# Expert weights of the second and third layer in runs of 16 KB a partition

## The chip, the core and the metric

One core of one Trainium2 chip. The time is that of one execution of the whole program on the device, in microseconds; the median of several runs is given, and less is better. The core has TensorE (PE), VectorE (DVE), ScalarE (ACT), GpSimd (POOL) and SyncE (SP), and 16 DMA engines that all queues share. Each engine works through its own instructions in order and meets the others by semaphores.

## What is computed

Three layers of a model on 256 tokens (and 256 of context), D = 1024, all in fp32. Each layer ends in 16 experts, and these are what the change touches:

```python
# second layer ("layer 1"): each token goes to two of 16 experts
def expert_block(args):
    xblk, e = args
    hid = jax.nn.silu(xblk @ w_gate[e]) * (xblk @ w_up[e])
    return hid @ w_down[e]
...
# third layer ("layer 2"): each expert takes its 32 best tokens
    top_aff, top_idx = lax.top_k(jnp.swapaxes(aff, 1, 2), cap)
    xe = jax.vmap(lambda hb, ib: hb[ib])(h, top_idx)
    hid = jax.nn.silu(jnp.einsum('becd,edf->becf', xe, w_e_gate)) * jnp.einsum('becd,edf->becf', xe, w_e_up)
    ye = jnp.einsum('becf,efd->becd', hid, w_e_down) * top_aff[..., None].astype(h.dtype)
```

Each `w_gate[e]`, `w_up[e]`, `w_down[e]` is 1024 x 1024, so an expert reads 12 MB of weights for at most 64 (layer 1) or 32 (layer 2) rows of tokens. The first layer ("layer 0") has experts of the same size; the change leaves their weights as they are.

## The kernel before

All weights go through one list, `W`, of pieces of at most 2 MB. `W.add` (L263 to L327) says which part of a weight a piece is and in what shape: `cols(w, n, k0, k, width)` takes `k` chunks of 128 rows and puts row 128 c + p on partition p, chunk c. An expert's matrix is two pieces, `h` = 0 and 1, of `k` = 4 chunks and the full width of 1024: on a partition, four rows of 4 KB each, which lie 128 rows apart in HBM. Layer 1 takes its pieces expert by expert in the order of `PAIRS` (gate 0, gate 1, up 0, up 1, down 0, down 1); layer 2 in four groups of four experts, all gates of a group, then all ups, then all downs. So 96 pieces each.

`W.place` gives each piece a place in SBUF: the ring of five, and in layer 1 four more (nine), in layer 2 three of the ring, four more, and one that serves once (eight). `sync_pieces` (L384) issues the DMAs from SP, in the order of the list, each after the piece that was in its place has been used up:

```python
            if before is not None and W.rows[before][1] == "pe":
                sp.wait_ge(*consumed(before))
...
            sp.dma_start(dst, src).then_inc(landed(n)[0], 16)
```

`consumed` is counted by TensorE after the last matmul on a piece.

Layer 1 does one expert at a time. The rows of tokens lie in `H`; TensorE picks an expert's 64 with a matrix of ones (`PS<-SM,H`), ACT copies them to `xeT` (L1912), TensorE multiplies them by gate into bank 0 and by up into bank 1 (`PS<-ring,xeT`, 32 matmuls a matrix of 512 columns, and each in two halves of 16, one a piece), ACT makes `hid` = silu(bank 0) (L1917), DVE multiplies bank 1 into it (L1942), TensorE turns `hid` (L1899), DVE copies it out as `hidT` (L1944), and TensorE multiplies by down (`PS<-ring,hidT`). Between up and the turning of `hid` TensorE picks the rows of the next expert. `H` was made before, from the turned-back activations in PSUM, by ACT (L1735).

Layer 2 does the same by groups: silu at L4030, the product at L4057, turned at L4010, copied out at L4060. Its token rows are split in two parts, `HH` (`H_high`, ACT, L3895) and `HL` (`H_low`, DVE, L3936), and a matrix of ones `SS` picks from both into `XE`, all before the first expert.

There are two more loops (the functions `late_...`, around L2014) for experts of layer 1 with more than 64 tokens; here they have no turn.

Outside the experts the kernel saves the turned activations to HBM and loads them back once, as one DMA of 128 partitions with 16 KB each: `act.dma_start(HT.rearrange("p c t -> p (c t)"), HD)` (L1231). It is issued from ACT.

Of the kernel before, what the change touches and what calls it, by code (L numbers as in the profile page):

```python
# [6 lines left out]
P = 128  # L7
D = 1024
NS = 5
SLOT = 8 * 512  # L10
F32 = mybir.dt.float32
# [3 lines left out]
ALU = mybir.AluOpType  # L15
ACT = mybir.ActivationFunctionType
# [154 lines left out]
def program(nc, I, out):  # L171
# [54 lines left out]
    def bank(i, n=1):  # L226
        return PS[:, i * 512:(i + n) * 512]
# [31 lines left out]
    W = Pieces()  # L259

    def cols(w, n, k0=0, k=8, width=512):
        return w[k0:k0 + k * P, n:n + width].rearrange("(c p) n -> p c n", p=P)

    ada, win, wo = I["ada_w"], I["even_w_in"][0], I["even_w_out"][0]
    moe = {"g": I["moe_w_gate"], "u": I["moe_w_up"], "d": I["moe_w_down"]}

# [32 lines left out]
    moe1 = len(W.rows)  # L299
    for e in range(16):  # L300
        for m, h in PAIRS:
            W.add((1, e, m, h), cols(moe[m][1, e], 0, k0=512 * h, k=4, width=D), "pe", k=4, width=D)
    end1 = len(W.rows)
    w2 = I["w_in_2"][0]
    W.add(("dt", 0), cols(w2, 4608, width=48), "pe", width=48)
# [16 lines left out]
    for g in range(4):  # L322
        for m in "gud":
            for e in range(4 * g, 4 * g + 4):
                for h in range(2):
                    W.add((2, e, m, h), cols(last_experts[m][0, e], 0, k0=512 * h, k=4, width=D), "pe", k=4, width=D)
    end2 = len(W.rows)  # L327
    W.place(range(NS), 0, end0)
    W.place(range(NS), end0, end1, extra=(5, 6, 7, 10), first=moe1 + NS)
# [1300 lines left out]
    def routed(layer, chunks, BL, zeroed, resume):  # L1630
        wide = BL == P
# [98 lines left out]
        def route_scalar():  # L1730
            def rows(ts):
                for t in ts:
                    c, g = divmod(t, 2)
                    act.wait_ge(*row_turned(t))
                    act.copy(H[:, c, 512 * g:512 * g + 512], bank(2 + t % 6)).then_inc(row_made.sem, 1)  # L1735

            ready_table(ACT.Sigmoid)
            act.wait_ge(*logits(0))
            act.activation(aff, bank(1)[:, 0:N], ACT.Sigmoid).then_inc(chance.sem, 1)
            rows(range(2 * nch))  # L1740
# [92 lines left out]
        def near_experts():  # L1833
# [80 lines left out]
            def near_scalar(m):  # L1914
                i = m % 2
                act.wait_ge(*weights(m, "g", 1)[2])
                act.activation(hid[i], bank(0), ACT.Silu).then_inc(silu.sem, 1)  # L1917
                if m < 15:
                    take_scalar(m + 1)
                act.wait_ge(*share_turned(m))  # L1920
                act.copy(shares_T[i], bank(1)[:, 0:2 * P]).then_inc(share_taken.sem, 1)
# [11 lines left out]
            def near_vector(m):  # L1933
                i = m % 2
                if m < 15:
                    if m:
                        dve.wait_ge(*x_turned(m - 1))
                    pick(m + 1, firsts)
                weigh(m)
                dve.wait_ge(*weights(m, "u", 1)[2])  # L1940
                dve.wait_ge(*silu(m))
                dve.tensor_tensor(hid[i], hid[i], bank(1), ALU.mult).then_inc(hidden.sem, 1)  # L1942
                dve.wait_ge(*h_turned(m))
                dve.tensor_copy(hidT[i].rearrange("p (h j) t -> p j h t", h=2),  # L1944
                                bank(3).rearrange("p (j h t) -> p j h t", j=4, h=2)).then_inc(h_taken.sem, 1)
                dve.wait_ge(*weights(m, "d", 1)[2])
                dve.wait_ge(*gate_taken(0))
                dve.tensor_tensor(yo[i], bank(2), gate_twice, ALU.mult).then_inc(y.sem, 1)
# [55 lines left out]
            def late_sync(m):  # L2004
                expert = nc.sync.value_load(OE[0:1, m:m + 1], min_val=0, max_val=15)
                if m == 0:
                    sp.wait_ge(*late_sent(2 * nch - 1))
                    sp.wait_ge(*consumed(end1 - 1))
                if m > 1:
                    sp.wait_ge(*late_x_turned(m - 2))  # L2010
                sp.dma_start(late_xe[m % 2][0:BL, :], XP[(m + 16) * BL:(m + 17) * BL, :]).then_inc(late_xe_in[m % 2].sem, 16)
                for k, (mt, h) in enumerate(PAIRS):
                    if k >= NS:
                        sp.wait_ge(*late_used(6 * m + k - NS))  # L2014
                    elif m:
                        sp.wait_ge(*late_used(6 * m - 6 + (k if k else NS)))
                    v = moe[mt][layer].rearrange("e (c p) n -> p e c n", p=P)
                    sp.dma_start(ring_t[:, k % NS * SLOT:(k % NS + 1) * SLOT].rearrange("p (e c n) -> p e c n", e=1, c=4),
                                 v[:, bass.ds(expert, 1), 4 * h:4 * h + 4, :]).then_inc(late_in[k % NS].sem, 16)

            def late_tensor(m):
                i = m % 2
# [16 lines left out]
            def late_scalar(m):  # L2039
                i = m % 2  # L2040
                act.wait_ge(*late_x_turned(m))
                act.copy(xeT[i], chunked(bank(3), 8)).then_inc(late_x_taken.sem, 1)
                act.wait_ge(*late_piece(m, "g", 1)[2])
                act.activation(hid[i], bank(0), ACT.Silu).then_inc(late_silu.sem, 1)
                act.wait_ge(*late_y(m))
                for h in range(2):
                    act.dma_start(YP[(m + 16) * 64:(m + 17) * 64, 512 * h:512 * h + 512],
                                  yo[i][64 * h:64 * h + 64, :]).then_inc(late_stored[i].sem, 16)
                act.wait_ge(*late_stored[i](2 * (m // 2) + 1))

            def late_vector(m):
                i = m % 2
                dve.wait_ge(*late_piece(m, "u", 1)[2])
                dve.wait_ge(*late_silu(m))
                dve.tensor_tensor(hid[i], hid[i], bank(1), ALU.mult).then_inc(late_hidden.sem, 1)
                dve.wait_ge(*late_h_turned(m))
                dve.tensor_copy(hidT[i].rearrange("p (h j) t -> p j h t", h=2),
                                bank(3).rearrange("p (j h t) -> p j h t", j=4, h=2)).then_inc(late_h_taken.sem, 1)
                dve.wait_ge(*late_piece(m, "d", 1)[2])
                if m > 1:  # L2060
                    dve.wait_ge(*late_stored[i](2 * (m // 2) - 1))
                dve.tensor_tensor(yo[i], bank(2), gate_twice, ALU.mult).then_inc(late_y.sem, 1)
# [1825 lines left out]
    def choice_scalar():  # L3888
        ready_table(ACT.Exp)
        act.wait_ge(*shifted(0))  # L3890
        act.activation(af, af, ACT.Exp).then_inc(af_exped.sem, 1)
        for t in range(4):
            c, g = divmod(t, 2)
            act.wait_ge(*row_turned(t))
            act.copy(HH[:, c, 512 * g:512 * g + 512], bank(ROW_BANKS[t])).then_inc(row_made.sem, 1)  # L3895
        for i in (1, 3, 5, 7):
            k = XE_BANKS[i]
            act.wait_ge(*xe_made(i))
            act.copy(XE[:, k, :], bank(k)).then_inc(odd_taken.sem, 1)

    def choice_vector():
# [30 lines left out]
        for t in range(4):  # L3932
            c, g = divmod(t, 2)
            sl = slice(512 * g, 512 * g + 512)
            dve.wait_ge(*row_made(t))
            dve.tensor_tensor(HL[c][:, sl], bank(ROW_BANKS[t]), HH[:, c, sl].bitcast(F32), ALU.subtract).then_inc(row_low.sem, 1)  # L3936
        dve.wait_ge(*picked(1))
        for c in xc:
            dve.tensor_tensor(SW[:, c, :, :], SS[:, c, :, :].bitcast(F32), a3[:, c, :].unsqueeze(2).to_broadcast([P, 16, 32]),
# [82 lines left out]
    def experts_scalar():  # L4022
# [4 lines left out]
        for g in range(4):  # L4027
            for h in range(2):
                act.wait_ge(*consumed(W.at[2, 4 * g + 3, "g", 1]))
                act.activation(hid[g % 2][:, h * 512:h * 512 + 512], bank(4 + h), ACT.Silu).then_inc(silu_.sem, 1)  # L4030
            if g == 0:
                act.wait_ge(*gate_spread(0))
                act.copy(gate_row, bank(2, 2)).then_inc(gate_taken.sem, 1)
            for h in range(2):
                act.wait_ge(*consumed(W.at[2, 4 * g + 3, "d", 1]))
                act.copy(YE[:, g, h * 512:h * 512 + 512], bank(4 + h)).then_inc(ye_taken.sem, 1)  # L4036
# [13 lines left out]
    def experts_vector():  # L4050
        for g in range(4):
            i = g % 2
            for h in range(2):
                t, sl = 2 * g + h, slice(h * 512, h * 512 + 512)
                dve.wait_ge(*consumed(W.at[2, 4 * g + 3, "u", 1]))
                dve.wait_ge(*silu_(t))
                dve.tensor_tensor(hid[i][:, sl], hid[i][:, sl], bank(6 + h), ALU.mult).then_inc(hidden.sem, 1)  # L4057
            for h in range(2):
                dve.wait_ge(*h_turned(2 * g + h))
                dve.tensor_copy(hidT[i][:, 4 * h:4 * h + 4, :], chunked(bank(6 + h), 4)).then_inc(h_taken.sem, 1)  # L4060
# [37 lines left out]
```

## Time and profile before

| | us |
|---|---|
| median of 3 runs | 2796.32 (2795.35 to 2801.36) |
| the profiled execution | 2797.12 |
| its span | 2795.7 |
| TensorE busy | 2388.2 (85%) |
| DMA queue q1 (SP's), share of 16 engines | 69.9% |

| Stretch, us from the start | what |
|---|---|
| 1397 to 1859 | experts of layer 1 |
| 1859 to 2317 | mixer of layer 2, choice of its tokens |
| 2317 to 2781 | experts of layer 2 |

A row of waits names the engine that waited, what it waited for and how long in total. The chain is followed back from the last instruction; a DMA in it is a stretch in which the engine behind it waited for a load. A group of a timeline lasts from its first start to its last end, waits within it included. For an SP group this means that its last issue ends at start + us.

### The profile page before, as it was taken

Reading aid. Unit: us, or ns where it says so; the run is one execution under the profiler, and the core shown is the slowest. Engines: PE = TensorE matmul, PEld = TensorE weight load, DVE = VectorE, ACT = ScalarE, POOL = GpSimd, SP = SyncE. Lnnn points to the kernel's source line nnn. Section 1 sums busy time; section 2 is a strip of 40 time slices with the busy share of each in tenths; the row PEclk is TensorE's granted clock in tenths of the full one; section 3 lists DMA queues with packets and bytes.
Section 4 is the critical chain, followed back from the end, with each engine's and each line's share of the span. In section 5 each row is a group of like instructions: output and inputs, shape, how many; then the busy total and the mean of one; then the engine's idle time right before and its main releaser. Section 6 shows DMA issues by size and latency. Waiting matters only on the chain.

```text
span 2795.7 us, 31565 instructions
## 1 busy us (share of the span) xinstructions
PE 2388.2 (85%) x12939; PEld 1475.5 (53%) x12939; DVE 1267.3 (45%) x2018; ACT 980.7 (35%) x1556; POOL 114.6 (4%) x171
## 2 busy tenths in 40 slices
PE   5977777589999999598899999879989969877776
PEld 3745655468888888463434343338677753211111
DVE  2478447579999999436311010025575451000001
ACT  3345323278888888314200000035444341000000
POOL 1010300100000000200000000000002000000000
PEclk8989899789999999699899999989999989999999
DMA  9279920289999998648499999973103558999997
GB/s 352 85 282 327 361 76 17 89 312 389 393 394 393 392 390 315 220 167 301 178 389 409 409 409 409 409 276 117 60 20 138 188 214 347 409 409 409 409 409 300
DMA packets 242411, 809.06 MB, mean 289 GB/s; under 512 B 10225, under 2 KB 10375, under 8 KB 241998
## 3 DMA queue, kind: packets, MB, share of 16 engines
q1 hardware_dynamic: 226688, 753.88, 69.9%
q0 software_dynamic: 12000, 37.16, 3.8%
q10 hardware_dynamic: 3568, 15.88, 1.4%
q8 instruction: 107, 1.75, 0.3%
q14 instruction: 48, 0.39, 0.0%
HBM read 775.28 MB, written 31.60 MB: 289 GB/s over the span
## 4 chain that ended last, share of the span: by engine, by line
PE 62%; DMA 20%; DVE 10%; ACT 3%; issue 2%; SPq 1%; DVEq 0%; POOL 0%; PEldq 0%; ACTq 0%; POOLq 0%
PE PS L256 60%; DMA ring<-in_w_e_down 6%; DMA ring<-in_moe_w_up 4%; DMA ring<-in_w_e_up 4%; DMA ring<-in_w_e_gate 3%; PE PS L2222 1%; DVE hgrn L1023 1%; SPq L394 1%; DMA ring<-in_moe_w_down 1%; DMA ring<-in_ada_w 1%; DVE hgrn L1013 1%; PE PS L570 1%; DVE SM L2858 0%; DVE SM L1491 0%; DVE cut L430 0%
## 5 line engine op out<-in xcount | busy, mean ns | idle before, releaser
L430 DVE TENSOR_TENSOR cut<-ring,cut 128x1024 fp32r<-128x1024 f32 x492 | 584.5, 1222 | 241.4 <-ACT cut L422 230.0
L422 ACT CAST cut<-ring 128x1024 fp32r<-128x1024 f32 x492 | 509.1, 1054 | 335.8 <-PE PS L256 306.9
L256 PE MATMUL PS<-cut,xeT 128*128 128x512 f32 x1536 | 364.7, 394 | 3.3 <-DVE cut L430 3.2
L256 PEld LDWEIGHTS PS<-cut,xeT 128*128 128x128 f32 x1536 | 285.8, 189 | 67.8 <-DVE cut L430 6.3
L256 PE MATMUL PS<-ring,XE 128*32 128x512 f32 x1008 | 224.1, 594 | 60.2 <-DMA ring<-in_w_e_up 35.8
L256 PE MATMUL PS<-ring,hidT 128*64 128x512 f32 (+1 forms) x1024 | 230.6, 599 | 45.4 <-DMA ring<-in_w_e_down 32.6
L256 PE MATMUL PS<-ring,xeT 128*64 128x512 f32 x1024 | 231.8, 603 | 14.7 <-DMA ring<-in_moe_w_gate 8.6
L256 PE MATMUL PS<-cut,parts 128*128 128x512 f32 x864 | 208.9, 403 | 27.9 <-DVE cut L430 18.2
L256 PE MATMUL PS<-parts,cut 128*128 128x512 f32 x864 | 204.7, 397 | 3.6 <-DVE cut L430 3.6
L256 PEld LDWEIGHTS PS<-cut,parts 128*128 128x128 f32 x864 | 166.9, 194 | 68.9 <-issue 16.5
L4057 DVE TENSOR_TENSOR X<-X,PS 128x512 f32<-128x512 f32 x8 | 5.1, 684 | 414.1 <-PE PS L256 414.1
L256 PEld LDWEIGHTS PS<-parts,cut 128*128 128x128 f32 x864 | 162.9, 190 | 39.3 <-issue 3.7
L256 PE MATMUL PS<-cut,hidT 128*128 128x512 f32 x768 | 179.4, 393 | 4.5 <-DVE hidT L2231 4.5
L256 PEld LDWEIGHTS PS<-ring,XE 128*32 128x32 f32 x1008 | 55.8, 109 | 225.2 <-issue 134.0
L256 PEld LDWEIGHTS PS<-ring,hidT 128*64 128x64 f32 (+1 forms) x1024 | 63.6, 124 | 199.4 <-issue 125.9
L256 PEld LDWEIGHTS PS<-cut,hidT 128*128 128x128 f32 x768 | 146.1, 190 | 35.3 <-DVE hidT L2231 4.7
L256 PEld LDWEIGHTS PS<-ring,xeT 128*64 128x64 f32 x1024 | 71.7, 138 | 169.8 <-issue 141.1
L1942 DVE TENSOR_TENSOR hid<-hid,PS 128x512 f32<-128x512 f32 x16 | 11.0, 689 | 249.1 <-PE PS L256 249.1
L4036 ACT COPY YE<-PS 128x512 f32<-128x512 f32 x8 | 4.3, 589 | 278.8 <-PE PS L256 278.8
L1917 ACT ACTIVATE hid<-PS 128x512 f32<-128x512 f32 x16 | 9.6, 597 | 231.8 <-PE PS L256 231.8
L256 PE MATMUL PS<-ring,CP 128*32 128x512 f32 x576 | 78.8, 651 | 4.0 <-DMA ring<-in_ada_w 2.9
L1912 ACT COPY xeT<-PS 128x512 f32<-128x512 f32 x16 | 9.4, 585 | 198.2 <-PE PS L256 198.2
(581 smaller groups left out, 2610.1 us busy)
## 6 DMA issues: line engine op xcount, KB each, us to landing
ring<-in_moe_w_gate SPq DMA_DIRECT2D x64, 2048.0 KB, 12.1
ring<-in_moe_w_up SPq DMA_DIRECT2D x64, 2048.0 KB, 12.1
ring<-in_moe_w_down SPq DMA_DIRECT2D x64, 2048.0 KB, 12.1
ring<-in_w_e_up SPq DMA_DIRECT2D x32, 2048.0 KB, 23.8
ring<-in_w_e_down SPq DMA_DIRECT2D x32, 2048.0 KB, 24.0
ring<-in_w_e_gate SPq DMA_DIRECT2D x31, 2048.0 KB, 23.8
ring<-in_ada_w SPq DMA_DIRECT2D x24, 2048.0 KB, 12.2
ring<-in_w_in SPq DMA_DIRECT2D x13, 2048.0 KB, 7.8
```

What stands on the lines that cost most here:

```text
L256: return pe.matmul(o, l, r, start=start, stop=stop, **kw)
L394: sp.dma_start(dst, src).then_inc(landed(n)[0], 16)
L422: act.copy(self.bufs[i % len(self.bufs)][0], w).then_inc(self.high.sem, 1)
L430: dve.tensor_tensor(low, w, high.bitcast(F32), ALU.subtract).then_inc(self.low.sem, 1)
L570: last = pe.transpose(bank(t)[:, 256 * j + c * P:256 * j + (c + 1) * P], U[:, 2 * r + c, k * P:(k + 1) * P], ident)
L1013: dve.tensor_tensor(n2(e), n2(cum), r_, ALU.subtract).then_inc(R["diff"].sem, 1)
L1023: ins = dve.tensor_tensor(level_view(w, l)[:, :, s, :], level_view(of, l)[:, :, s, :], level_view(e, l)[:, :, s, :], ALU.mult)
L1912: act.copy(xeT[m % 2], chunked(bank(0), 8)).then_inc(x_taken.sem, 1)
L1917: act.activation(hid[i], bank(0), ACT.Silu).then_inc(silu.sem, 1)
L1942: dve.tensor_tensor(hid[i], hid[i], bank(1), ALU.mult).then_inc(hidden.sem, 1)
L2222: last = pe.transpose(bank(6 + t % 2)[:, i * P:(i + 1) * P], src[:, i * P:(i + 1) * P], ident)
L4057: dve.tensor_tensor(hid[i][:, sl], hid[i][:, sl], bank(6 + h), ALU.mult).then_inc(hidden.sem, 1)
```

## The change

The four rows that a partition holds of an expert's piece are now neighbours in HBM: partition p has rows 4p to 4p + 3 of the piece's 512, which is one run of 16 KB on both sides. This is done for all pieces of layers 1 and 2 (and in the `late_` loops), by `four_rows`. Chunk c of a piece now holds rows 4p + c in place of 128 c + p. What is multiplied by it must have its rows in the same order. So where token rows or `hid` are copied out of a bank, 512 elements are read with a step of four (`by_fours`) and written in order (`in_order`): L1735, L1917, L1942 in layer 1, L3895, L3936, L4030, L4057 in layer 2. The turning, and everything after it, is unchanged.

```diff
+    def four_rows(w, h):
+        return w[512 * h:512 * h + 512, :].rearrange("(p c) n -> p c n", c=4)
+
+    def by_fours(a):
+        return a.rearrange("p (n f) -> p f n", f=4)
+
+    def in_order(a):
+        return a.rearrange("p (f n) -> p f n", f=4)
...
-            W.add((1, e, m, h), cols(moe[m][1, e], 0, k0=512 * h, k=4, width=D), "pe", k=4, width=D)
+            W.add((1, e, m, h), four_rows(moe[m][1, e], h), "pe", k=4, width=D)
...
-                    W.add((2, e, m, h), cols(last_experts[m][0, e], 0, k0=512 * h, k=4, width=D), "pe", k=4, width=D)
+                    W.add((2, e, m, h), four_rows(last_experts[m][0, e], h), "pe", k=4, width=D)
...
-                    act.copy(H[:, c, 512 * g:512 * g + 512], bank(2 + t % 6)).then_inc(row_made.sem, 1)
+                    row = H[:, c, 512 * g:512 * g + 512]
+                    if wide:
+                        act.copy(row, bank(2 + t % 6)).then_inc(row_made.sem, 1)
+                    else:
+                        act.copy(in_order(row), by_fours(bank(2 + t % 6))).then_inc(row_made.sem, 1)
...
-                act.activation(hid[i], bank(0), ACT.Silu).then_inc(silu.sem, 1)
+                act.activation(in_order(hid[i]), by_fours(bank(0)), ACT.Silu).then_inc(silu.sem, 1)
...
-                dve.tensor_tensor(hid[i], hid[i], bank(1), ALU.mult).then_inc(hidden.sem, 1)
+                dve.tensor_tensor(in_order(hid[i]), in_order(hid[i]), by_fours(bank(1)), ALU.mult).then_inc(hidden.sem, 1)
...
-                    v = moe[mt][layer].rearrange("e (c p) n -> p e c n", p=P)
+                    v = moe[mt][layer].rearrange("e (a p c) n -> p e a c n", a=2, c=4)
...
-            act.copy(HH[:, c, 512 * g:512 * g + 512], bank(ROW_BANKS[t])).then_inc(row_made.sem, 1)
+            act.copy(in_order(HH[:, c, 512 * g:512 * g + 512]), by_fours(bank(ROW_BANKS[t]))).then_inc(row_made.sem, 1)
...
-            dve.tensor_tensor(HL[c][:, sl], bank(ROW_BANKS[t]), HH[:, c, sl].bitcast(F32), ALU.subtract).then_inc(row_low.sem, 1)
+            dve.tensor_tensor(in_order(HL[c][:, sl]), by_fours(bank(ROW_BANKS[t])), in_order(HH[:, c, sl].bitcast(F32)),
+                              ALU.subtract).then_inc(row_low.sem, 1)
...
-                act.activation(hid[g % 2][:, h * 512:h * 512 + 512], bank(4 + h), ACT.Silu).then_inc(silu_.sem, 1)
+                act.activation(in_order(hid[g % 2][:, h * 512:h * 512 + 512]), by_fours(bank(4 + h)), ACT.Silu).then_inc(silu_.sem, 1)
...
-                dve.tensor_tensor(hid[i][:, sl], hid[i][:, sl], bank(6 + h), ALU.mult).then_inc(hidden.sem, 1)
+                dve.tensor_tensor(in_order(hid[i][:, sl]), in_order(hid[i][:, sl]), by_fours(bank(6 + h)), ALU.mult).then_inc(hidden.sem, 1)
```

No instruction is added, removed or moved on any engine; line numbers grow by 11 and more. What changes in the order is the shape of the copies. On SP, at the start of layer 2's pieces, before (the last numbers are partitions x rows x elements of one DMA):

```order
L394 DMA ring_49<-in_w_out 128x8x512 x2
L394 DMA ring_49<-in_w_e_gate 128x4x1024 x5
L394 DMA ring_21812<-in_w_e_gate 128x4x1024
L394 DMA ring_21813<-in_w_e_gate 128x4x1024
L394 DMA YE_21803<-in_w_e_gate 128x4x1024
L394 DMA ring_49<-in_w_e_up 128x4x1024 x5
```

and in the changed kernel, the same place:

```order
L405 DMA ring_49<-in_w_out 128x8x512 x2
L405 DMA ring_49<-in_w_e_gate 128x4096 x5
L405 DMA ring_21812<-in_w_e_gate 128x4096
L405 DMA ring_21813<-in_w_e_gate 128x4096
L405 DMA YE_21803<-in_w_e_gate 128x4096
L405 DMA ring_49<-in_w_e_up 128x4096 x5
```

The rows stand as they stood; each expert piece has become one run a partition, and a piece in another shape (`in_w_out`) is as before.

## Rows read from the trace of the kernel before

**Rows 1.** Page, slices of 69.9 us: DMA busy tenths, GB/s, packets.

```profile
DMA  9279920289999998648499999973103558999997
GB/s 352 85 282 327 361 76 17 89 312 389 393 394 393 392 390 315 220 167 301 178 389 409 409 409 409 409 276 117 60 20 138 188 214 347 409 409 409 409 409 300
DMA packets 242411, 809.06 MB, mean 289 GB/s; under 512 B 10225, under 2 KB 10375, under 8 KB 241998
```

**Rows 2.** Waits of TensorE, 2317 to 2790 us: waited for: us, times, longest.

```profile
PE PS L256 <- DMA ring<-in_w_e_up: 35.8, 24, 1.6
PE PS L256 <- DMA ring<-in_w_e_down: 32.6, 23, 1.5
PE PS L256 <- DMA ring<-in_w_e_gate: 23.6, 18, 1.5
```

**Rows 3.** Timelines of SP: start us, us until the group's last issue ends.

```profile
1373.59 29.71 SPq L394 DMA_DIRECT2D ring<-in_moe_w_up  x2
...
2321.25 30.15 SPq L394 DMA_DIRECT2D ring<-in_w_e_up  x8
```

**Rows 4.** Chain that ended last, its end: start us, us, what.

```profile
2753.41 23.50 DMA ring<-in_w_e_down
2776.96 3.65 PE PS L256 x16
```

**Rows 5.** DMA view, window 2400 to 2700 us: packets, queue q1.

```profile
DMA packets 30879, 122.77 MB, mean 409 GB/s; under 512 B 931, under 2 KB 931, under 8 KB 30870
...
q1 hardware_dynamic: 30870, 122.63, 102.4%
```

**Rows 6.** Chain that ended last, second layer's experts.

```profile
1418.14 26.60 PE PS L256 x136
...
1640.80 22.91 PE PS L256 x104
1663.72 2.17 SPq L394
...
1854.99 3.68 PE PS L256 x16
```

**Rows 7.** Windows: stretch, us, busy PE, PEld, DVE, ACT, POOL, PEclk, DMA share, GB/s.

```profile
1397.30:1640.80 243.50, 238.40 (x1238) 102.02 (x1238) 25.29 (x66) 15.26 (x28) 0.00 (x0) 0.99 1.01 403
```

**Rows 8.** Waits of TensorE, 1397 to 1860 us.

```profile
PE PS L256 <- DMA ring<-in_moe_w_gate: 8.6, 6, 2.7
PE PS L256 <- DMA ring<-in_moe_w_up: 5.4, 5, 1.1
...
PE PS L256 <- DMA ring<-in_moe_w_down: 0.3, 1, 0.3
```

**Rows 9.** DMA view, window 286.5 to 288 us: packets, queue q10.

```profile
DMA packets 40, 0.66 MB, mean 437 GB/s; under 512 B 0, under 2 KB 0, under 8 KB 0
...
q10 hardware_dynamic: 40, 0.66, 101.8%
```

**Rows 10.** Groups by form: xcount | busy us, mean ns | idle before.

```profile
L1023 DVE TENSOR_TENSOR hgrn<-Q,hgrn 128x256 f32<-128x256 f32 x56 | 23.3, 417 | 3.4 <-ACT hgrn L1085 3.3
...
L3392 DVE TENSOR_TENSOR state<-state,XW 128x256 f32<-128x256 f32 x24 | 10.2, 425 | 0.8
```

**Rows 11.** Timeline, expert 8 of the second layer, around hid.

```profile
1663.74 0.69 DVE L1942 TENSOR_TENSOR hid<-hid,PS 128x512 f32<-128x512 f32 x1 [14.52 <-PE PS L256]
...
1667.24 0.61 PE L1899 MATMUL PS<-KC,hid 128*128 128x128 f32 x4
```

**Rows 12.** Timelines ahead of the third layer's experts.

```profile
2291.85 1.93 PE L256 MATMUL PS<-X,SM 128*32 128x256 f32 x16 [1.20 <-DMA SM<-in_w_router]
...
2306.28 2.48 DVE L3936 TENSOR_TENSOR H_low<-PS,H_high 128x512 fp32r<-128x512 f32 x4
...
2310.00 3.21 PE L256 MATMUL PS<-SS,H_low 128*128 128x512 f32 x8
```

**Rows 13.** Window around the whole load `HT<-HD`.

```profile
284.50:291.50 7.00, 0.00 (x0) 0.00 (x0) 6.61 (x18) 1.70 (x3) 0.00 (x0) 0.54 0.97 375
```

More of the change, by code:

```diff
@@ L2016, in late_sync @@
                         sp.wait_ge(*late_used(6 * m - 6 + (k if k else NS)))
-                    v = moe[mt][layer].rearrange("e (c p) n -> p e c n", p=P)
+                    v = moe[mt][layer].rearrange("e (a p c) n -> p e a c n", a=2, c=4)
                     sp.dma_start(ring_t[:, k % NS * SLOT:(k % NS + 1) * SLOT].rearrange("p (e c n) -> p e c n", e=1, c=4),
-                                 v[:, bass.ds(expert, 1), 4 * h:4 * h + 4, :]).then_inc(late_in[k % NS].sem, 16)
+                                 v[:, bass.ds(expert, 1), h, :, :]).then_inc(late_in[k % NS].sem, 16)
             def late_tensor(m):
@@ L2043, in late_scalar @@
                 act.wait_ge(*late_piece(m, "g", 1)[2])
-                act.activation(hid[i], bank(0), ACT.Silu).then_inc(late_silu.sem, 1)
+                act.activation(in_order(hid[i]), by_fours(bank(0)), ACT.Silu).then_inc(late_silu.sem, 1)
                 act.wait_ge(*late_y(m))
@@ L2054, in late_vector @@
                 dve.wait_ge(*late_silu(m))
-                dve.tensor_tensor(hid[i], hid[i], bank(1), ALU.mult).then_inc(late_hidden.sem, 1)
+                dve.tensor_tensor(in_order(hid[i]), in_order(hid[i]), by_fours(bank(1)), ALU.mult).then_inc(late_hidden.sem, 1)
                 dve.wait_ge(*late_h_turned(m))
```

## The prediction

> **What bounds the kernel now.** First the page's slices: the DMA row shows where the 16 DMA engines are full, and the row under it at which rate [rows 1]. Counted from one, slices 10 to 15 (389 to 394 GB/s) are the experts of the first layer, which the change leaves alone; slices 21 to 26 are those of the second ("layer 1"), 35 to 40 those of the third ("layer 2"), both at a flat 409 in the middle, and these are what it touches. Then who waits there.
>
> Layer 2 is plain. From the first piece that TensorE frees to the last landing, TensorE waits 92.0 us for weights (35.8, 32.6 and 23.6) [rows 2]. SP issues the first piece of the running stream at 2321.25 [rows 3], and the last one lets TensorE go on at 2776.96 [rows 4]: 455.7 us for 88 pieces of 2 MB (96, less the 8 for which places stand free beforehand). A 300 us window inside it moved 409 GB/s [rows 5], so a piece takes 2097.2 KB / 409.1 = 5.126 us, 88 of them 451.1 us, and 4.6 us are start and landing. The stream is the bound; TensorE has 92 us to spare.
>
> Layer 1 has two halves. Up to 1663.72 the chain is TensorE alone: one expert's period is (1640.80 - 1418.14) / 8 = 27.83 us [rows 6], TensorE is busy 238.4 of 243.5 us, and the DMA engines run full beside it at 403 GB/s [rows 7]. Six pieces take 6 x 5.126 = 30.8 us, 3.0 us more than TensorE needs, so the nine places run dry, and from 1663.72 on the chain alternates with SP and the DMA queue. Three rows of waits say what that costs TensorE: 8.6 + 5.4 + 0.3 = 14.3 us [rows 8]. From the period it is a little more: expert 15 would begin its down product at 1418.14 + 15 x 27.83 = 1835.6 and its second half 3.6 later, at 1839.2; it began at 1854.99 [rows 6], 15.8 us late.
>
> **The change, part by part.** (1) *One run of 16 KB a partition in place of four of 4 KB.* The bytes and the number of DMAs stay; each DMA has 128 runs in place of 512. That the two inner dimensions really become one shows in SP's order above, on both sides of the copy. The price of a run: in the 300 us window q1 has 30870 packets, 931 of them small ones that only signal, so 29939 of 4 KB; 300 us x 16 engines x 1.024 / 29939 = 0.164 us each [rows 5]. Since they overlap a little (102.4%), the rate gives 4096 B x 16 / 409.1 = 0.160 us. The kernel already has packets of 16 KB: `HT<-HD` loads a contiguous 2 MB with 16 KB a partition, on ACT's queue, the same kind of queue. In 1.5 us where nothing else ran, 40 of them took 1.5 x 16 x 1.018 / 40 = 0.611 us each [rows 9], less than four times 0.160 = 0.640. I take the same 4 ns of overlap off: 0.607 us. A piece is then 8 x 0.607 + 0.005 for the signal = 4.86 us, 431 GB/s. Bounds: 0.611 without overlap gives 4.90; the 437 GB/s of that short window gives 4.80.
>
> The Trainium skill has a rule that speaks against any gain ("DMA: Bandwidth & Descriptors", section Bandwidth): for loads from HBM the HBM side binds, at about 358 GB/s, so the length of a run would buy nothing. Here the trace disagrees with the figure: 409 GB/s over 300 us. By that rule the sum would be 0; by the rows it is 0.27 us a piece.
>
> *Layer 2*: 88 x (5.126 - 4.86) = **23.4 us** less, all on the path, since TensorE still has 69 us of waits left. Bounds 88 x 0.23 = 20.2 and 88 x 0.33 = 28.7.
>
> *Layer 1*: the stream restarts when TensorE frees the first place, at 1373.59 + 29.71 = 1403.3 [rows 3], with 87 pieces to go. Before: 87 x 5.126 = 445.9, plus 5.8 for start and landing, is 1854.99. Now: 87 x 4.86 = 422.8 + 5.8, so the last piece lands at 1831.9, and TensorE wants it at 1839.2. Six pieces take 29.2 us against the 27.83 of the period, and the stock lasts to the end with some 7 us left (4 us at the slow bound). So the layer becomes TensorE's throughout: the stream would give 23.1 us, but only **15.8 us** can be had (14.3 by the waits alone). This cut-off is the one place where the two layers differ.
>
> (2) *Reading a bank with a step of four.* Silu and the product with it, 16 of each in layer 1 and 8 in layer 2, and the copies of token rows. Counts and elements stay. No row of before has a step inside a bank. The nearest: the last level of hgrn reads and writes every second element of SBUF, and its whole group of 128x256 takes 417 ns against 425 ns for a contiguous one [rows 10]. I take nothing, from that row; the other end is four times as long. In layer 1 DVE's product starts at 1663.74 and takes 0.69, TensorE transposes it at 1667.24 [rows 11]: 2.8 us of cover by the picks of the next expert; four times as long (2.8) it still fits. Silu has a whole product of 32 matmuls as cover. In layer 2 the boundary between groups is covered by the 69 us. The one place without cover: four subtractions L3936, 2.48 us from 2306.28, whose result TensorE takes at 2310.00 [rows 12]; 1.2 us of slack, so twice as long costs 1.3 us, four times 6.2, and nothing after it hides this, for the stream restarts only when TensorE has freed a piece. In layer 1 the row copies are over well before the first pick reads them. Term: 0, up to 6.2.
>
> The Trainium skill ("Advanced Engine Details and Errata", section Memory Cachelines) says that PSUM has lines of two fp32 values and that every two consecutive elements should be contiguous. No row here shows such a read; by that rule the copies would come out towards twice as long, the 1.3 us above.
>
> (3) *Small loads beside the stream.* The router's weights come by the software queue beside q1 in both layers, and TensorE waits for them (1.20 us at 2291.85) [rows 12]. A packet there now waits behind one of 0.61 in place of 0.16 us: 0.45 us each, perhaps twice; two layers, so **+1.3 us** (0.9 to 1.8).
>
> Sum: -23.4 - 15.8 + 1.3 = -37.9. The profiled execution took 2797.12 (span 2795.7), so it would take 2759.2; the median of the runs is 0.8 lower, so 2758.4, I say 2758. The pieces of layer 0 keep 4 KB, and the SP queue, which now holds four times the data for as many runs, will issue as soon as a place is free; neither moves a bound.
>
> **Rivals.** (A) *The steps cost*: 16 KB packets work, but reading a bank with steps takes up to four times as long, deciding at L3936. Then 2764.6 (+6.2). For it: no row with a step of four in PSUM; against: the step of two is free in SBUF. A price of this kind is in my range.
>
> (B) *The change does not reach the rate*: the runs are cut to 4 KB again, or the load from HBM is held at 409 by something other than the packet. For it: the flatness of 406 to 412 in every slice, and only 1.5 us of evidence. Against: 409 is exactly what 0.160 us a packet gives. Then 2796.3 + 0 to 2 = 2797.
>
> (C) *Slower: 16 KB reads get in each other's way.* If a packet takes over 0.640 us, the change loses in both layers. The whole load `HT<-HD`, with other queues beside it, ran at 375 GB/s [rows 13]; were that the pattern's own rate, a piece would take 5.59 us, layer 2 88 x 0.466 = 41 us more, layer 1 about as much (87 x 0.466, less the idle at its start, 38): 2796 + 79 = 2875. Against: the lower rate lies where others share the engines, and the clean part is at 437.
>
> **How the numbers follow.** Forecast, with the small costs within it: 0.83. A: 0.08. B: 0.05. C: 0.04. Ends of the range: fast 2796.3 - 28.7 - 15.8 = 2752; slow 2796.3 - 20.2 - 14.3 + 1.8 + 6.2 = 2770, which takes in A. A change within 0.2% (5.6 us) is about what a measurement of this kernel can't tell from none; B falls there, but for 0.01 of it with the costs of A. Faster 0.91, same 0.04, slower 0.05.
>
> **What would show it.** The packets of 8 KB and over should rise from 242411 - 241998 = 413 [rows 1] to about 25,000 (192 x 128), of 0.61 us each; the flat slices should read 430 in layer 2. In layer 1 the three waits for weights should be gone, the chain TensorE alone with a period of 27.83 us to the end, and the DMA rows no longer full there. In layer 2 SP's first free piece to the last landing should be 432 us, and the waits for weights some 69 us. L3936 should keep its 2.48 us for four, and L1942 its 0.69. A layer 1 that still waits for weights in its last experts would say that the stock argument is off by more than 7 us; a period over 27.83 would say that the steps reach TensorE; a rate near 409 says B.

## The result and the profile after

| | before | changed |
|---|---|---|
| median | 2798.84 us (4 runs, 2795.35 to 2802.98) | 2764.24 us (4 runs, 2756.68 to 2766.94) |
| ratio | 1 | 0.9872 (95% interval 0.9853 to 0.9891) |
| profiled execution | 2797.12 us | 2756.68 us |

34.6 us by the medians, 40.4 by the two profiled executions. One execution of runs_8k (below) took 3597.1 us at a mean granted clock of 0.64, where all others lay between 0.94 and 0.95; it is left out of every figure. The changed kernel's page first, with the row of rates that answers to [rows 1] (slices of 68.9 us):

```profile
span 2755.2 us, 31565 instructions
...
GB/s 361 83 285 320 373 84 1 73 297 392 389 395 393 391 394 380 155 171 373 108 388 428 427 428 427 428 318 123 62 1 129 193 172 359 428 427 429 427 428 308
DMA packets 168683, 809.06 MB, mean 294 GB/s; under 512 B 10225, under 2 KB 10375, under 8 KB 143694
```

The flat stretches of layers 1 and 2 read 427 to 429 GB/s in place of 409, those of layer 0 are as before. The packets of 8 KB and over went from 413 to 168683 - 143694 = 24989. The DMA view of 300 us in layer 2, which answers to [rows 5]:

```profile
DMA packets 8814, 128.39 MB, mean 428 GB/s; under 512 B 978, under 2 KB 978, under 8 KB 978
...
q1 hardware_dynamic: 8806, 128.26, 100.5%
```

7828 packets of 16 KB (8806 less 978 small ones) took 300 x 16 x 1.005 / 7828 = 0.616 us each. The queue moved 128.26 MB in 300 us, 427.5 GB/s, or 4.905 us a piece.

Layer 1, the chain that ended last (compare [rows 6]), start us, us, what:

```profile
1416.59 26.61 PE PS L256 x136
...
1806.26 22.91 PE PS L256 x104
1831.38 7.11 PE PS L256 x32
```

Expert 0's down product starts at 1416.59, expert 14's at 1806.26: 14 periods of 27.83 us, as before the change while it still had a stock. No SP and no load of a weight stands in the chain of this layer any more, and TensorE's waits from 1390 to 1865 us have no row with a weight in them, where [rows 8] had three. The row of 1831.38 is expert 15. It comes 25.1 us after expert 14's, not 27.83: there is no expert 16 whose rows are to be picked.

Layer 2: SP's first issue into a freed place, and the last landing (compare [rows 3, 4]):

```profile
2300.01 30.11 SPq L405 DMA_DIRECT2D ring<-in_w_e_up  x8
```

```profile
2736.53 3.65 PE PS L256 x16
```

The waits of TensorE for weights there (compare [rows 2]; us, times, longest):

```profile
PE PS L256 <- DMA ring<-in_w_e_up: 30.5, 24, 1.4
PE PS L256 <- DMA ring<-in_w_e_down: 24.2, 20, 1.3
PE PS L256 <- DMA ring<-in_w_e_gate: 18.7, 15, 1.3
```

436.5 us in place of 455.7, and 73.4 us of waits in place of 92.0. The reads with a step, where [rows 11, 12] had 0.69 and 2.48 us:

```profile
L1957 DVE TENSOR_TENSOR hid<-hid,PS 128x512 f32<-128x512 f32 x16 | 11.0, 688 | 230.6 <-PE PS L256 230.6
```

```profile
2272.12 1.07 PE L256 MATMUL PS<-X,SM 128*32 128x256 f32 x16 [2.21 <-DMA SM<-in_w_router]
...
2286.02 2.48 DVE L3951 TENSOR_TENSOR H_low<-PS,H_high 128x512 fp32r<-128x512 f32 x4
```

Both copies keep their times. The row at 2272.12 is another matter: TensorE waits 2.21 us for layer 2's router weights, where it was 1.20.

**The stages.** Every trace can be cut at four events: SP's first issue into a freed place in layer 1; the end of expert 15's down product on TensorE; SP's first issue into a freed place in layer 2; the end of the matmuls on the last piece. The kernels of this study (runs_8k_b stands for runs_8k too), in us:

| kernel | ahead | layer 1 | between | layer 2 | tail | span |
|---|---|---|---|---|---|---|
| before | 1403.3 | 455.3 | 462.6 | 459.3 | 15.1 | 2795.7 |
| changed | 1401.7 | 436.75 | 461.5 | 440.15 | 15.0 | 2755.2 |
| again | 1411.6 | 436.75 | 462.6 | 440.1 | 15.1 | 2766.1 |
| again_2 | 1410.6 | 436.7 | 465.1 | 440.2 | 15.0 | 2767.6 |
| l2_only | 1403.7 | 455.4 | 463.3 | 440.1 | 15.1 | 2777.6 |
| l1_only | 1408.8 | 436.75 | 461.5 | 459.1 | 15.1 | 2781.2 |
| steps_only | 1406.2 | 455.5 | 459.8 | 459.3 | 15.0 | 2795.8 |
| packets_4k | 1403.6 | 456.2 | 466.0 | 459.7 | 15.1 | 2800.6 |
| runs_8k_b | 1403.4 | 442.7 | 465.1 | 446.4 | 15.1 | 2772.7 |
| queue_5 | 1405.0 | 436.75 | 465.2 | 439.9 | 15.1 | 2761.9 |
| router_first | 1407.4 | 436.7 | 464.7 | 440.0 | 15.1 | 2763.9 |
| router_both | 1401.0 | 436.75 | 462.7 | 440.15 | 15.1 | 2755.7 |
| both_2 | 1403.3 | 436.7 | 461.1 | 440.0 | 15.1 | 2756.1 |

The change is worth 18.6 us in layer 1 and 19.2 in layer 2. Among kernels whose loads of a layer have the same length of run, its stage repeats to 0.3 us; packets_4k alone is longer, by 0.9 us in layer 1 and 0.4 in layer 2. What spreads is the rest, by 10 us ahead of layer 1 and 6 between the layers. Between the two traces of the changed kernel most of the first was there before the changed part of the program begins: the load `HT<-HD`, whose way there is the same in all kernels, is issued at 279.4 us in changed and 286.7 in again (283.4 in before), 7.3 of the 9.9 us.

### The profile page after: what moved, and what is told of

Same layout as the page of the kernel before. It is cut to its first block, busy times and chain, and to the rows that moved or that the text cites. A ratio compares the mean times of both kernels' runs of the same rounds, so it can differ in the third digit from the quotient of the medians.

```text
span 2755.2 us, 31565 instructions
## 1 busy us (share of the span) xinstructions
PE 2386.1 (87%) x12939; PEld 1480.3 (54%) x12939; DVE 1266.8 (46%) x2018; ACT 981.3 (36%) x1556; POOL 116.1 (4%) x171
## 2 busy tenths in 40 slices
DMA packets 168683, 809.06 MB, mean 294 GB/s; under 512 B 10225, under 2 KB 10375, under 8 KB 143694
## 4 chain that ended last, share of the span: by engine, by line
PE 70%; DMA 13%; DVE 10%; ACT 3%; issue 2%; SPq 1%; DVEq 0%; POOL 0%; ACTq 0%; POOLq 0%; PEldq 0%
PE PS L256 67%; DMA ring<-in_w_e_up 6%; DMA ring<-in_w_e_down 4%; PE PS L2237 1%; DVE hgrn L1034 1%; DMA ring<-in_ada_w 1%; DVE hgrn L1024 0%; DVE SM L2873 0%; SPq L405 0%; DVE cut L441 0%; DVE hidT L1959 0%; PE PS L581 0%; DMA HT<-HD 0%; DVE SM L1502 0%; DVE gate_sums L870 0%
## 5 line engine op out<-in xcount | busy, mean ns | idle before, releaser
L256 PE MATMUL PS<-ring,hidT 128*64 128x512 f32 (+1 forms) x1024 | 230.4, 602 | 36.5 <-DMA ring<-in_w_e_down 24.2
L256 PEld LDWEIGHTS PS<-cut,parts 128*128 128x128 f32 x864 | 166.8, 194 | 69.9 <-issue 18.2
L256 PEld LDWEIGHTS PS<-cut,hidT 128*128 128x128 f32 x768 | 145.2, 189 | 35.1 <-DVE hidT L2246 4.7
L1932 ACT ACTIVATE hid<-PS 128x512 f32<-128x512 f32 x16 | 9.6, 597 | 219.8 <-PE PS L256 219.8
## 6 DMA issues: line engine op xcount, KB each, us to landing
ring<-in_w_e_down SPq DMA_DIRECT2D x32, 2048.0 KB, 30.6
```

What stands on the lines that cost most here:

```text
L256: return pe.matmul(o, l, r, start=start, stop=stop, **kw)
L1932: act.activation(in_order(hid[i]), by_fours(bank(0)), ACT.Silu).then_inc(silu.sem, 1)
```

## Experiments

### The changed kernel once more (again, again_2)

No edit.

> The changed kernel once more, as it is, for the spread of its runs and a second trace. My account: layer 1 (expert layer of the second layer) is TensorE's alone, period 27.83 us an expert, no wait for weights; layer 2 (third layer) is the stream's, 88 pieces at 428 GB/s, 436.5 us from SP's first free place to TensorE going on with the last piece; 36 to 41 us below the kernel before. Rival: one of the two stages does not repeat, and then the 10 us between the profiled run (2756.7) and the other runs (2762 to 2767) lie in it: a stream at under 425 GB/s in layer 2, or waits for weights in layer 1.

> The changed kernel, as it is, on the same chip and in the same rounds as the kernel of the next run. Account: median 2762 to 2765, stretch from layer 1's router issue to the first free place 33.5 us, layer stretches 436.75 and 440.1.

Measured: 2762.49 us (ratio 0.9862, 0.9846 to 0.9879) and 2764.63 us (0.9876, 0.9854 to 0.9897). Both layer stages repeat, so the spread between single executions is not theirs. From the issue of layer 1's router weights to the first free place it took 33.6 us in both, 31.8 in the first trace of the changed kernel and 30.9 in before's. That is taken up below.

### One layer alone (l1_only, l2_only)

```diff
# l2_only; l1_only is the other way round
-            W.add((1, e, m, h), four_rows(moe[m][1, e], h), "pe", k=4, width=D)
+            W.add((1, e, m, h), cols(moe[m][1, e], 0, k0=512 * h, k=4, width=D), "pe", k=4, width=D)
...
-                act.activation(in_order(hid[i]), by_fours(bank(0)), ACT.Silu).then_inc(silu.sem, 1)
+                act.activation(hid[i], bank(0), ACT.Silu).then_inc(silu.sem, 1)
```

and the same for the layer's other copies.

> Runs of 16 KB and the steps in layer 1 alone; layer 2 as before. Account: waits for weights in layer 1 fall from 14.3 us to 0 and the stage shortens by 18.4 us (from the first free place to the second half of expert 15's down product); layer 2's stream stays at 409 GB/s and 455.7 us; the whole is 17 to 20 us below before, although 87 pieces x 0.22 us are 19 us as well, so the cap by TensorE is told by the trace (DMA engines no longer needed at full rate at the end), not by the total. Rival: layer 1's gain comes with layer 2's state: under 12 us.

> Runs of 16 KB and the reads with a step of four in layer 2 alone; layer 1 as before. Account (packet price): layer 2 gives 455.7 - 436.5 = 19 us, layer 1 keeps its 14.3 us of waits for weights and begins to wait around expert 8; the whole is 18 to 20 us below the kernel before. Rival (the two gains hang together, for instance because layer 1 hands over earlier or the queue is left in another state): not additive, under 15 or over 24 us.

Measured: l1_only 2782.77 us (0.9941, 0.9924 to 0.9957), 16.2 below before; l2_only 2779.85 us (0.9928, 0.9912 to 0.9945), 19.1 below. Together 35.3, against 36.5 for both in the same comparison (again). Each layer has its gain in its own stage (18.6 and 19.2 us) and leaves the other's to 0.2 us: two gains, added. The 16.2 us of l1_only are less than the 17 to 20 expected, though its stage gave the whole 18.6; the rest lies in the stages that spread, and the interval reaches from 12 to 21 us.

### The reads with a step alone (steps_only)

```diff
-            W.add((1, e, m, h), four_rows(moe[m][1, e], h), "pe", k=4, width=D)
+            W.add((1, e, m, h), cols(moe[m][1, e], 0, k0=512 * h, k=4, width=D), "pe", k=4, width=D)
...
-                    W.add((2, e, m, h), four_rows(last_experts[m][0, e], h), "pe", k=4, width=D)
+                    W.add((2, e, m, h), cols(last_experts[m][0, e], 0, k0=512 * h, k=4, width=D), "pe", k=4, width=D)
```

> The banks are read with a step of four as in the changed kernel, but the weights stay in four rows 128 apart, 4 KB each; the sums over rows therefore pair wrong rows, nothing is left out and the work is the same in kind and amount. Account: the steps cost nothing: L3936 and its like keep 2.48 us for four, the product with silu 0.69, the whole is within 2 us of before. Rival (lines of PSUM): longer copies, up to 4 times; then up to 6 us slower, all of it ahead of layer 2's experts.

Measured: ratio 1.0003 (0.9992 to 1.0013). Of its groups by form, the one at issue:

```profile
L1957 DVE TENSOR_TENSOR hid<-hid,PS 128x512 f32<-128x512 f32 x16 | 11.0, 687 | 250.0 <-PE PS L256 250.0
```

687 ns with a step of four in PSUM, 689 without (one of them in [rows 11], 0.69). The step costs nothing on DVE, and silu on ACT (L1932) keeps its 597 ns too. Rival A is out.

### Neighbouring rows, but 4 KB packets (packets_4k)

```diff
     def four_rows(w, h):
-        return w[512 * h:512 * h + 512, :].rearrange("(p c) n -> p c n", c=4)
+        return w[512 * h:512 * h + 512, :].rearrange("(p c) n -> p c n", c=4)[:, ::-1, :]
...
             dst, _ = piece(next_key[n])
+            if moe1 <= n < end1 or moe2 <= n:
+                dst = dst[:, ::-1, :]
```

> The changed kernel, but each DMA names the four rows of a partition from the last to the first on both sides, so that they can't become one run: neighbouring rows in HBM as in the change, the same result, 512 runs of 4 KB in place of 128 of 16 KB. Account (price of a packet): the gain goes: packets of 0.164 us, 409 GB/s, layer 2's stretch 455 us again, waits for weights in layer 1 about 14 us, the whole within 3 us of before. Rival (the order of the rows in HBM makes the loads faster): 428 GB/s and 36 us below before, though the packets are 4 KB.

Measured: ratio 1.0006 (0.9995 to 1.0016). Its DMA view of 2400 to 2700 us:

```profile
DMA packets 30879, 122.77 MB, mean 409 GB/s; under 512 B 932, under 2 KB 932, under 8 KB 30870
...
q1 hardware_dynamic: 30870, 122.63, 102.4%
```

That is [rows 5] to the packet, with the new order of rows in HBM. Its waits for weights in layer 1 are back too: 9.6 us for gate, 6.5 for up, 0.7 for down.

The gain lies in the length of the run and in nothing else of the change: not in which rows are read together, not in the copies. (For the order of the rows to matter after all, naming them backwards would have to cost just what it brings; that each packet costs what [rows 5] had speaks against it.)

### Runs of 8 KB (runs_8k, runs_8k_b)

```diff
     def four_rows(w, h):
-        return w[512 * h:512 * h + 512, :].rearrange("(p c) n -> p c n", c=4)
+        return w[512 * h:512 * h + 512, :].rearrange("(a p b) n -> p a b n", a=2, b=2)
     def by_fours(a):
-        return a.rearrange("p (n f) -> p f n", f=4)
+        return a.rearrange("p (a n f) -> p a f n", a=2, f=2)
```

> Two neighbouring rows a partition in place of four, twice: 256 runs of 8 KB a piece, banks read with a step of two in two halves. Account: a fixed price per packet, from 4 KB (32 packets an engine, 5.126 us) and 16 KB (8 packets, 4.906 us a piece) (5.126 - 4.906) / 24 = 0.0092 us; 16 packets give 4.98 us, 421 GB/s; layer 2's stretch 455.7 - 88 x 0.147 = 442.8 us; layer 1: six pieces 29.9 us against 27.83, stock lasts to about the last expert, so nearly the whole 18 us; total 28 to 32 us below before. Rival (all or nothing: only one run a partition is fast): 409 GB/s, total within 3 us of before; or 8 KB is as good as 16 KB: 428 GB/s, 36 to 40 us below.

> The kernel with runs of 8 KB once more, for a trace: its times lay 20 to 29 us below before, less than the 28 to 32 I had worked out. Account 1 (a fixed price per packet, and the rest is scatter of stages that the change doesn't touch): 421 GB/s, layer 2 from first free place to the end of the last piece 459.3 - 13 = 446.3 us (before 459.3, with 16 KB 440.1), layer 1 from first free place to the end of expert 15 at 437 to 439 us (455.3 and 436.75). Account 2 (8 KB is worth less than half of the way, the price isn't linear in packets): 415 GB/s or less, layer 2 at 452 us or more and layer 1 at 445 or more.

Measured: 2773.8 us (runs_8k; 0.9912, 0.9896 to 0.9929) and 2774.69 us (runs_8k_b; 0.9913, 0.9897 to 0.9930), 24.1 and 22.8 below before where 28 to 32 were expected. The rows of runs_8k_b:

```profile
DMA packets 16385, 126.43 MB, mean 421 GB/s; under 512 B 960, under 2 KB 960, under 8 KB 960
...
q1 hardware_dynamic: 16376, 126.29, 101.1%
```

In layer 1 TensorE waits 2.5 us for gate, 1.6 for up and 0.5 for down.

421 GB/s and 446.4 us for layer 2, both as the fixed price per packet says. Layer 1 took 442.7 us, 4 more than account 1 gave it. There I had judged the stock by eye; worked out as in the prediction it is 87 x 4.98 + 5.8 = 439.1 us after the first free place. TensorE wants the last piece 433.2 us after it (1831.38 + 3.55 - 1401.72 in the changed kernel), so it comes 5.9 us late. Measured: 442.65 - 436.75 = 5.9. So 8 KB is worth two thirds of 16 KB in layer 2 (12.9 of 19.2 us) and in layer 1 too (12.7 of 18.6), there because the stock runs out shortly before the end. The two stages make 25.6 us; in the profiled execution the stretch between them took 2.5 us back (465.1 for 462.6).

### A queue no deeper than before (queue_5)

```diff
             dst, _ = piece(next_key[n])
+            if moe1 + 5 <= n < end1 or moe2 + 5 <= n:
+                sp.wait_ge(*landed(n - 5))
```

> The changed kernel, but SP issues a piece of layers 1 and 2 only when the piece five ahead of it has landed, so that the queue never holds more than five pieces, as many as before the change by the times to landing (24 us = 4.7 pieces); with 16 KB packets it had come to 30.6 us = 6.2 pieces in layer 2. Account: the depth is worth nothing, the packets are: 428 GB/s, within 2 us of the changed kernel. Rival (SP, held up by a full queue before, was the bound and the gain is its earlier issue): most of the gain goes, 15 us or more above the changed kernel.

Measured: 2764.57 us (0.9885, 0.9867 to 0.9903); the median time to landing in layer 2 went back from 30.6 to 24.4 us, and the stages stayed at 436.75 and 439.9 us. In the middle of layer 2 an issue of SP's took 4.9 us (median of `in_w_e_up`) before the change, and takes 0.33 us in the changed kernel and in this one: that SP could issue earlier is not where the gain comes from. What holds an issue up for 4.9 us no run here shows.

### The router's weights first (router_first, router_both, both_2)

```diff
# layer 2 (router_first)
         after_meeting(sp, after_mix)
+        sp.wait_ge(*rw_in(0))
         sync_pieces(moe2 + 3, end2)
# layer 1 as well (router_both, both_2)
         sp.wait_ge(*mod_out(5))
-        sync_pieces(moe1 + NS, end1)
...
         route_gpsimd()
+        if layer:
+            sp.wait_ge(*rw_in(0))
+            sync_pieces(moe1 + NS, end1)
```

> The changed kernel, but in layer 2 SP holds back the last five pieces issued ahead of the experts until the router's weights (64 KB) have landed. In the changed kernel TensorE waits 2.21 us for them (1.20 before the change). Account (they wait behind packets of the stream, 0.61 us in place of 0.16): the wait falls under 0.5 us, the stretch between the experts of layers 1 and 2 shortens by about 2 us, and the five pieces (24.5 us) are there in time. Rival (the wait is GpSimd's own issue, 4.7 us from issue to first packet): unchanged at about 2.2 us. Counter-effect to look for: the first pieces come later and TensorE waits for them at the start of layer 2. The total can't tell 2 us; the trace can.

> The changed kernel with the router's weights ahead of the stream in both layers: in layer 2 as in the run before, in layer 1 SP holds back the pieces after the fifth until they have landed. In seven traces the stretch from the issue of layer 1's router weights to the first free place takes 30.8 to 31.2 us where TensorE waits 0.3 to 0.7 us for them, and 33.4 to 33.8 where it waits 1.4 to 1.8; in the second kind TensorE's granted clock reads 0.82 where the first reads 1.00. Account: the late router load costs its wait and, through the lower clock that follows, as much again; without it the stretch is 31 us or less also with 16 KB packets, 2.5 us less than in the last run, and layer 1's own stretch stays 436.75 us. Rival: the clock falls for another reason, and the stretch stays at 33.5 us with the wait gone. If the held pieces come too late, TensorE waits for weights in the first expert and the 436.75 us grow. In total 2 to 3 us below the changed kernel, which five rounds hardly tell.

> The kernel with the router's weights ahead of the stream in both layers, once more, beside the changed kernel. Account (late router load and the lower clock after it): 3 to 6 us below the run before it, stretch to the first free place at 31 us or less. Rival (the last run's 2757.0 was the luck of the stages ahead, whose length spreads over 7 us): the same median within 2 us.

Measured: router_first 2765.78 us (0.9886, 0.9869 to 0.9902); router_both 2757.01 us (0.9852, 0.9833 to 0.9871); both_2 2760.17 us (0.9864, 0.9841 to 0.9887) beside again_2's 2764.63 on the same chip.

In layer 2 the load lands 2.9 us after its issue in place of 7.8, and TensorE's row now names ACT, with the 1.20 us of [rows 12]:

```profile
2279.41 1.93 PE L256 MATMUL PS<-X,SM 128*32 128x256 f32 x16 [1.20 <-ACT X L527]
```

So in before the load and ACT had come at about the same time, and its lateness cost nothing; with 16 KB packets TensorE starts on these matmuls up to 1 us later (7.8 us after the issue of the load in place of 6.9). The price is not a function of the packet alone: packets_4k waited 3.1 us there. Nor is the wait GpSimd's own way to the first packet (4.7 us in changed): with the stream held back the whole load lands after 2.9. The wait did not fall under 0.5 us, as expected, because ACT is awaited there as well.

Of that 1 us nothing is left at the end. From the issue of this load to the first free place in layer 2 it takes 36.3 us in before, 35.7 in changed, 35.6 in again, 36.5 in again_2, and with the load first 36.3 in router_first, 34.9 in router_both and 36.4 in both_2. The stretch between the layers, expected about 2 us shorter, is 464.7 us in router_first, longer than in changed (461.5) and again (462.6). The rows above show part of the reason: behind a wait of 2.21 us in changed the 16 matmuls take 1.07 us, behind one of 1.20 us in before and in router_first they take 1.93. The granted clock of the 5 us around them is 0.84 in changed (from 2269.29 us) and 0.50 in before (from 2289.93) and in router_first (from 2277.48).

In layer 1 it costs more than its wait. again and router_both at the same place, the matmuls that make the logits on TensorE:

```profile
1385.78 1.37 PE L256 MATMUL PS<-HT,SM 128*32 128x256 f32 x16 [1.53 <-DMA SM<-in_router_w]
...
1387.99 0.87 PE L256 MATMUL PS<-KC,logit_parts 128*128 128x16 f32 x4
```

```profile
1376.81 1.07 PE L256 MATMUL PS<-HT,SM 128*32 128x256 f32 x16 [0.20 <-ACT HT L527]
...
1378.51 0.62 PE L256 MATMUL PS<-KC,logit_parts 128*128 128x16 f32 x4
```

After a wait of 1.53 us these 20 matmuls take 1.37 + 0.87 us, and the 16 between and behind them, which turn the token rows, 1.11 + 2.04; after none for the load it is 1.07 + 0.62 and 0.66 + 1.51. The second and third stretch of 5 us from the issue of the load on (busy us of each engine, the granted clock, DMA share, GB/s), first again:

```profile
1383.00:1388.00 5.00, 3.47 (x27) 1.53 (x26) 1.22 (x6) 2.51 (x4) 0.53 (x1) 0.84 0.98 366
1388.00:1393.00 5.00, 2.92 (x19) 2.78 (x18) 3.79 (x20) 2.26 (x5) 0.00 (x0) 0.82 1.02 431
```

and router_both:

```profile
1375.40:1380.40 5.00, 4.75 (x44) 3.00 (x42) 2.66 (x11) 3.74 (x8) 0.53 (x1) 1.00 0.84 308
1380.40:1385.40 5.00, 0.39 (x5) 0.28 (x4) 3.97 (x23) 0.91 (x2) 0.00 (x0) 1.00 1.01 399
```

In the first stretch both have a granted clock of 0.66. Then it is 0.84 and 0.82 where router_both (and before) has 1.00 and 1.00, so part of that stretch of again ran at the lower of TensorE's two levels, after an engine idle for 1.53 us. Of the 3.0 us between the two traces (33.6 and 30.6 us to the first free place) 1.4 are the later start on the logits, and 0.6 come at the other end, where it takes 6.7 us in place of 6.1 from the first matmul on the first piece until its place is free; the rest lies between, where DVE's routing follows the logits. The stretch from that issue to the first free place is 33.4 to 33.8 us in again, again_2, l1_only, queue_5 and router_first (16 KB; waits of 1.4 to 1.8 us), 31.8 in the first trace of the changed kernel (0.9), and 30.8 to 31.2 in before, l2_only, packets_4k and runs_8k_b (0.3 to 0.7). steps_only, with 4 KB packets, has 33.5 and a wait of 1.5: the wait goes with it, not the packet as such. With the load first it is 30.6 us in both traces, with 16 KB packets. Held-back pieces cost nothing: layer 1 keeps 436.75 us.

That the lower clock follows from the wait is what these traces suggest for layer 1, and it is not a rule: in layer 2 the 16 matmuls take 1.07 us behind waits of 1.31 (l1_only) and 2.21 us (changed), and 1.93 behind waits of 1.20 (before) and 2.16 us (l2_only).

On the same chip both_2's median is 4.5 us below again_2's, of which the traces account for 3.0, all in layer 1; their four runs don't overlap (2757.56 to 2763.20 and 2764.20 to 2769.10), though the two intervals against before do. By the medians it is the fastest version here.

## Where the prediction was right and where not

The time, 2764.2, lies in the range of 2752 to 2770, 6 us above the number. The mechanism held in both layers; three terms were mis-sized, and two of them cancel. The total alone would have told a wrong story: nearest to it of all the numbers in the prediction is that of rival A, 2764.6, whose mechanism is absent.

- *What bounds the kernel.* Right, and shown by l1_only and l2_only.
- *The price of a packet.* The step "I take the same 4 ns of overlap off" failed: 0.613 us by the rate and 0.616 by the share, not 0.607; a piece takes 4.905 us, not 4.86. The bound of 4.90, which took the row as it stood, was the better value. Layer 2: 19.2 us, not 23.4.
- *Layer 1 becomes TensorE's throughout.* Right, with 27.83 us an expert to the end. The size was off by a step I left out: I carried the period on to expert 15, but its last stretch has no pick of a next expert, 2.7 us shorter. TensorE wanted its pieces earlier than I said, and the gain is 18.6 us, not 15.8. The same slip made the margin of the stock look larger (TensorE's time for the last piece is 1403.3 + 433.2 = 1836.5 in before's time, not 1839.2). Together with the slower packet it used up the 7 us of stock: by the rates the last piece lands at 1401.7 + 87 x 4.905 + 5.8 = 1834.2, and TensorE starts on it at 1834.9. In the trace it lands 36.4 us after its issue at 1797.9, at 1834.3, and the weight load of TensorE waits 0.3 us for it. So it sufficed by a hair, which was luck, and the 18.6 us are almost all that the stream had to give as well. One sign of the prediction went against its own sum: with 29.2 us of loads against 27.83 the DMA engines stay full in layer 1, and they do (427 to 429 GB/s).
- *The steps.* Nothing taken, nothing found.
- *Small loads.* 1.3 us taken. The waits grew by 1.8 us, the upper end of my range (with 16 KB packets in the layer from 0.45 to 1.5 us on average in layer 1, from 1.20 to 2.0 in layer 2), but I had taken the waits for the cost. In layer 1 the lower clock came with a late load, and the stretch grew by 2.5 to 2.9 us in five of six traces with 16 KB packets there. In layer 2 the stretch did not grow with the wait. The term is about 2.7.
- *The sum.* -18.6 - 19.2 + 2.7 = -35.1, against 34.6 by the first medians and 36.5 and 35.5 by the later ones. My -37.9 had the two layers right by luck, by errors that cancel (39.2 for 37.8), and half of the third term.
- *Rivals.* A fell to steps_only. B fell to the rate; my argument against it, that 409 is exactly what 0.160 us a packet gives, was none, for the 0.160 had been worked out from the 409. C fell: 0.616 us is below 0.640. The 375 GB/s of [rows 13] are not the pattern's own rate, since the stream of the same packets runs at 427.5; that the other queues beside it took the rest is likely and not shown.

What stays open: why the stages ahead of the changed part spread by up to 10 us from one execution to the next, and what decides the clock behind the router's load. The first trace of the changed kernel had 0.9 us of wait in layer 1, a granted clock of 0.50 in its third stretch of 5 us, and lost 1 us only; and layer 2 had the two clocks the other way round.

## What to carry to other kernels

Here a load in which each partition gets one contiguous run of 16 KB in place of four of 4 KB moved 428 in place of 409 GB/s; where a stream of weights is the bound, reorder the contraction so that neighbouring rows share a partition, and let the copies out of PSUM, which have to be made anyway, bring the other operand into the same order. Count the gain only up to the next bound, with the last turn of the loop worked out by itself. And when the stream is made to fill the engines better, look at the small loads that TensorE waits for and try them ahead of it, but judge by the whole stretch and not by the wait: in layer 1 a start 1.4 us later on the logits went with a stretch 3.0 us longer, in layer 2 one 1 us later with none.

## What the runs showed of the hardware

- Three lengths of packet on one queue, each in a 300 us window: 4 KB 409.1, 8 KB 421, 16 KB 427.5 GB/s; a piece of 2 MB in 5.126, 4.98 and 4.905 us with 32, 16 and 8 packets on each engine. That is a straight line: 9.2 ns for each packet and 4.83 us for the bytes, 434 GB/s. The Trainium skill ("DMA: Bandwidth & Descriptors", section Bandwidth) has both parts: a fixed cost of about 3 cycles for each packet, and 435 GB/s as what the 16 ports can take. The traces agree with the second; the first, at the 850 MHz that the section gives for the ports, would be 3.5 ns, an estimate, and the traces show 9.2. Its 358 GB/s for loads from HBM, in which the prediction saw a rule against any gain, are by the same section each core's half when both cores of a pair stream; here one core runs, at 409 to 428 GB/s.
- A copy out of PSUM with a step of four elements takes what one without a step takes, on DVE (687 and 689 ns for 128x512) and on ACT (597 and 597). The Trainium skill ("Advanced Engine Details and Errata", section Memory Cachelines) wants every two consecutive elements contiguous; for these two engines no run here shows that it matters.
- A DMA whose rows are named in descending order on both sides runs at the rate of its 4 KB packets, 409 GB/s.
